# Two stacked transformer kinds on one core: the gated feed-forward hidden row made transposed, with head and end reordered

## The chip, the cores and the metric

The program runs on one core of one Trainium2 chip. The metric is the device time in microseconds of one execution; the lower, the better. TensorE is called PE, its weight load PEld, VectorE DVE, ScalarE ACT, GpSimd POOL and the DMA-issuing SyncE SP. L515 is line 515 of the kernel before.

## The reference, cut to what matters

A sequence of 256 rows of width 1024 goes through two layers of a first kind and then two layers of a second kind, everything in float32. Of a layer of the first kind only the feed-forward half is touched by the main part of the change (D_FF is 2816):

```python
def rms_norm(x, g):
    y = xf * lax.rsqrt(jnp.mean(xf * xf, axis=-1, keepdims=True) + EPS)
    return (y * g.astype(jnp.float32)).astype(x.dtype)
...
        x = x + jnp.concatenate([ret, da], axis=-1) @ w_out[l]
        h = rms_norm(x, ffn_norm_g[l])
        x = x + (jax.nn.silu(h @ w_gate[l]) * (h @ w_up[l])) @ w_down[l]
```

The second kind ends with `x = x + jnp.square(jax.nn.relu(hf @ w_up)) @ w_down` (its hidden width is 4096), and the program ends with a last rms norm. The row scale of a norm (the rsqrt) is one number for each of the 256 rows.

## The kernel before, in words

**Products.** Every float32 weight and activation is split into a high and a low part, and a product is the sum hi*hi + hi*lo + lo*hi. Weights come in slabs of 1 MB: 4 k-tiles of 128 by 512 columns (`w_raw`, `w_hi`, `w_lo`, a ring of 4). SP loads a slab as two DMAs when `lo_ready` says that the ring's place is free, ACT copies it to `w_hi` (`split_hi`, L1097), DVE subtracts for `w_lo` (`split_lo`, L1626), PE uses it. Three slabs are split ahead of their use (AHEAD = 3). The ACT and DVE programs are in-order lists in which the splits are written between the other work (`splits(n)`).

**Row-wise products** (`slab_product`, L515 to L517). The activations hT (transposed, hi and lo, k on the partitions) are stationary, the weights move, 512 columns at a time: for each k-tile and each of the two row halves three matmuls. The result has the sequence rows on its partitions. A block is an accumulation over all k-tiles into a pair of banks; there are two pairs, and `open_block` waits on `acc_free` until the block two before it has been read out.

**Transposed products** (`hidden`, L1032 to L1035), in the second kind only: the weights are stationary, and the moving operand is hi and lo of x side by side (512 columns) against the high weights, and x hi alone (256 columns) against the low weights. The result has hidden features on its partitions and the sequence along the columns. A bank then holds hi*hi plus the low-weight term in its left half and hi*lo in its right half: ACT copies the right half (`cross2`, L1563), DVE adds (`L2179`).

**The first kind's gated row before.** A wide block makes 256 gate columns and 256 up columns from two slabs (`gate_up` in SP's list: left half gate, right half up). ACT takes silu of the gate half with the row scale (L1342), DVE multiplies the up half by row scale and gate (L1904) into `hid1`. PE turns it with four transposes one block later (`turn_hid1`, L561), ACT takes the high part (L1120), DVE the low part (L1651). There are 11 wide blocks for each layer, then the down product over 22 k-tiles (6 slabs for each 512 columns), which `add_x` adds to x.

**Around it.** Before the gated row, w_out's product ends (`half_product`, L544 to L546). x's second half is added, turned by eight transposes (`turn_x(1)`), taken by ACT and DVE (L1127, L1655) and squared (L1137), DVE makes the mean (L1675), and POOL the reciprocal root (L2250), which is `rstd_ready`.

**Head.** After the constants have landed PE turns the gain rows, runs filler matmuls (`fill`, L631; a fill is two PE instructions), turns x's first half, runs a small sum, turns a group of convolution rows, and fills again; then the first projection starts (`first_pair`). Slab 0 is split in two halves. **End.** The last block is made one row half at a time; row half 0 is scaled by ACT (L1602), row half 1 by DVE in two pieces (L2234), and three DMAs write it out (SP L487, ACT L1604, SP L489).

Of the kernel before, what the change touches and what calls it, by code (L numbers as in the profile page):

```python
# [28 lines left out]
P = 128  # L29
# [9 lines left out]
FILLS = (4, 5, 4)  # L39
# [26 lines left out]
UPS = FF2 // HALF  # L66
BLOCKS1, BLOCKS2 = 7 + 2 + 11 + 2, 5 + 2 + 16 + 2 + UPS + 2
TURNS1, TURNS2 = 4 + 4 + 4 + 4 + 4 + 4 + 4 + 11 + 4 + 1, 2 + 1 + 1 + 10 + 12 + 1 + 1 + 4 + 4 + 4
assert not (BLOCKS1 % 2 or TURNS1 % 2 or TURNS2 % 2)
# [123 lines left out]
def build(nc, t, out):  # L193
    with ExitStack() as ctx:
# [60 lines left out]
        gate1 = over("gate1", [P, R, HALF], 44)  # L255
        hid1 = over("hid1", [P, R, HALF], 46)
# [62 lines left out]
        first_rest = sem("first_rest")  # L319
# [40 lines left out]
        cross_ready = sem("cross_ready")  # L360
        hid_ready = sem("hid_ready")
# [25 lines left out]
        def _(sp):  # L387
            q = Place(sp)
            sp.dma_start(x[:, 0, 0:NB], t["x"].rearrange("b (r p) d -> p (b r) d", p=P)[:, 0, 0:NB]).then_inc(x_in, 16)
# [22 lines left out]
            def halves(w, k0, c0):  # L412
                src = w[k0 * P:(k0 + 4) * P, bass.ds(c0, HALF)]
                return src.rearrange("(c p) n -> p c n", p=P)

            for l in q.layers(dict(slab=len(KTS1))):
                w = {n: t[n][bass.ds(l, 1)].rearrange("o k n -> (o k) n")
                     for n in ("w_in", "w_out", "w_gate", "w_up", "w_down")}
                for k0 in (0, 4):
                    for c0 in COLS1[:2]:  # L420
                        slab(*rows(w["w_in"], k0, 4, c0, NB))
                sp.wait_ge(first_rest, 1)
# [66 lines left out]
            sp.dma_start(rows_out[:, 1, 0:NB], outrow[:, 1, 0:NB]).then_inc(out_done, 16)  # L489
# [4 lines left out]
        def _(pe):  # L494
# [12 lines left out]
            def slab_product(a, hi, lo, kts, cols, first, last, halfway=None):  # L507
# [3 lines left out]
                for j, kt in enumerate(kts):  # L511
# [6 lines left out]
                    if j == 1 and halfway:  # L518
                        halfway()
# [64 lines left out]

            def first_block(product, cols=NB):
# [8 lines left out]
                product(a, hT_hi, hT_lo, range(0, 4), cols, True, False, turn_rest)  # L594
# [3 lines left out]
            def first_pair(product):  # L598
# [9 lines left out]
                def all_of_first():  # L608
                    pe.wait_ge(turn_free, turned_to + 1)
                    pe.wait_ge(first_rest, 1)  # L610

                product(a[0], hT_hi, hT_lo, range(0, 4), NB, True, False, all_of_first)
# [4 lines left out]
                for b in range(2):  # L617
                    product(a[b], hT_hi, hT_lo, range(4, 8), NB, False, True)

# [26 lines left out]
            for l in q.layers(dict(slab=len(KTS1), blk=BLOCKS1, turn=TURNS1, scores=16, dve=9)):  # L646
# [113 lines left out]
                first_pair(slab_product)  # L760
# [37 lines left out]
                def turn_hid1(blk):  # L798
                    read_out(blk)
                    turn_group([(hid1[:, r, c * P:(c + 1) * P], c * SEQ + r * P)  # L800
                                for c in range(2) for r in range(R)])
# [6 lines left out]
                earlier, last = q.now("turn"), q.now("blk")  # L808
                for b in range(2):
                    a = open_block()  # L810
                    for n in range(6):
# [3 lines left out]
                        if (b, n) == (0, 5):  # L815
                            all_turned()
# [1554 lines left out]
```

## Time and profile before

| what | value |
|---|---|
| median of 3 runs | 1441.19 us (1439.85 to 1441.36) |
| the profiled execution: its time | 1439.99 us |
| its span, first to last instruction | 1438.2 us |
| mean granted TensorE clock | 0.999 |
| PE / PEld / DVE / ACT / POOL busy | 99 / 82 / 65 / 52 / 7 % of the span |

The profiled execution's time is 1.8 us more than its span; the difference of a span is taken over to the time as it is. A matmul's own duration in the trace (0.39 us for 512 columns) overlaps with the next one; what one costs on PE is the distance from its start to the start of the next.

### The profile page before, as it was taken

Reading aid. Unit: us, or ns where it says so; the run is one execution under the profiler, and the core shown is the slowest. Engines: PE = TensorE matmul, PEld = TensorE weight load, DVE = VectorE, ACT = ScalarE, POOL = GpSimd, SP = SyncE. Lnnn points to the kernel's source line nnn. Section 1 sums busy time; section 2 is a strip of 40 time slices with the busy share of each in tenths; the row PEclk is TensorE's granted clock in tenths of the full one; section 3 lists DMA queues with packets and bytes.
Section 4 is the critical chain, followed back from the end, with each engine's and each line's share of the span. In section 5 each row is a group of like instructions: output and inputs, shape, how many; then the busy total and the mean of one; then the engine's idle time right before and its main releaser. Section 6 shows DMA issues by size and latency. Waiting matters only on the chain.

```text
span 1438.2 us, 19054 instructions
## 1 busy us (share of the span) xinstructions
PE 1425.9 (99%) x7027; PEld 1185.8 (82%) x7027; DVE 941.4 (65%) x1165; ACT 745.9 (52%) x994; POOL 100.0 (7%) x116
## 2 busy tenths in 40 slices
PE   8999999999999999999999999999999999999997
PEld 7788888888788888888888888888888888888886
DVE  6766655446757555446799878764467998787642
ACT  6665544345855444336665445544266654455431
POOL 1211000002111000000220000000002200000001
PEclk9999999999999999999999999999999999999999
DMA  8533755454434755465355566555553555665550
GB/s 336 176 119 117 234 179 198 165 189 163 158 118 149 231 175 182 168 205 187 126 184 175 184 205 208 200 180 201 175 186 127 183 176 184 205 207 200 181 187 29
DMA packets 172646, 257.11 MB, mean 179 GB/s; under 512 B 8478, under 2 KB 90400, under 8 KB 172448
## 3 DMA queue, kind: packets, MB, share of 16 engines
q1 hardware_dynamic: 169408, 249.36, 51.7%
q10 hardware_dynamic: 3023, 6.28, 1.3%
q8 instruction: 45, 0.74, 0.2%
q0 software_dynamic: 144, 0.52, 0.1%
q14 instruction: 26, 0.20, 0.0%
HBM read 255.08 MB, written 1.05 MB: 178 GB/s over the span
## 4 chain that ended last, share of the span: by engine, by line
PE 95%; POOL 1%; DVE 1%; issue 1%; ACT 1%; DMA 0%; POOLq 0%; DVEq 0%; ACTq 0%
PE bank L515 23%; PE bank L517 23%; PE bank L516 23%; PE bank L1033 8%; PE bank L561 4%; PE bank L1032 4%; PE bank L544 1%; PE bank L546 1%; PE bank L545 1%; PE bank L699 1%; POOL cst L2309 1%; PE bank L890 1%; PE bank L656 1%; PE bank L682 1%; PE bank L1035 1%
## 5 line engine op out<-in xcount | busy, mean ns | idle before, releaser
L1626 DVE TENSOR_TENSOR w_lo<-w_raw,w_hi 128x2048 fp32r<-128x2048 f32 (+2 forms) x247 | 538.3, 2184 | 215.8 <-ACT w_hi L1097 212.9
L1097 ACT CAST w_hi<-w_raw 128x2048 fp32r<-128x2048 f32 (+2 forms) x247 | 448.7, 1825 | 231.6 <-PE bank L517 207.8
L515 PE MATMUL bank<-w_hi,hT 128*128 128x512 f32 (+1 forms) x1056 | 417.7, 396 | 0.0
L517 PE MATMUL bank<-w_hi,hT 128*128 128x512 f32 (+1 forms) x1056 | 410.9, 389 | 0.0
L516 PE MATMUL bank<-w_lo,hT 128*128 128x512 f32 (+1 forms) x1056 | 410.1, 388 | 0.0
L517 PEld LDWEIGHTS bank<-w_hi,hT 128*128 128x128 f32 x1056 | 198.2, 188 | 41.2
L515 PEld LDWEIGHTS bank<-w_hi,hT 128*128 128x128 f32 x1056 | 198.4, 188 | 40.3 <-issue 2.5
L516 PEld LDWEIGHTS bank<-w_lo,hT 128*128 128x128 f32 x1056 | 198.6, 188 | 38.0
L1033 PE MATMUL bank<-hT,w_hi 128*128 128x512 f32 x512 | 178.2, 396 | 0.2
L1032 PE MATMUL bank<-hT,w_lo 128*128 128x256 f32 x448 | 125.2, 279 | 0.0
L1033 PEld LDWEIGHTS bank<-hT,w_hi 128*128 128x128 f32 x512 | 94.4, 188 | 21.0 <-DVE sum L2179 0.9
L2250 POOL TENSOR_TENSOR stat<-stat,cst 128x2 f32<-128x2 f32 (+4 forms) x24 | 44.8, 1869 | 959.6 <-DVE stat L1675 830.8
L515 PE MATMUL bank<-w_hi,hid2T_hi 128*128 128x512 f32 x240 | 93.5, 389 | 0.0
L517 PE MATMUL bank<-w_hi,hid2T_lo 128*128 128x512 f32 x240 | 93.4, 389 | 0.0
L516 PE MATMUL bank<-w_lo,hid2T_hi 128*128 128x512 f32 x240 | 93.4, 389 | 0.0
L1032 PEld LDWEIGHTS bank<-hT,w_lo 128*128 128x128 f32 x448 | 84.4, 188 | 1.3
L515 PE MATMUL bank<-w_hi,hid1T_hi 128*128 128x512 f32 x176 | 69.0, 392 | 0.0
L517 PE MATMUL bank<-w_hi,hid1T_lo 128*128 128x512 f32 x176 | 68.6, 389 | 0.0
L516 PE MATMUL bank<-w_lo,hid1T_hi 128*128 128x512 f32 x176 | 68.5, 389 | 0.0
L1120 ACT CAST hid1T_hi<-bank 128x512 f32 (+1 forms) x22 | 12.9, 587 | 90.3 <-PE bank L561 90.3
L1655 DVE SCALAR_TENSOR_TENSOR hT<-bank,gcols,hT 128x256 fp32r<-128x256 f32 (+1 forms) x72 | 32.6, 507 | 38.5 <-ACT hT L1127 35.5
L1563 ACT COPY cross<-bank 128x256 f32<-128x256 f32 x64 | 20.8, 377 | 70.8 <-PE bank L1033 70.8
(269 smaller groups left out, 1597.9 us busy)
## 6 DMA issues: line engine op xcount, KB each, us to landing
w_raw<-in_w_gate SPq DMA_DIRECT2D x108, 512.0 KB, 3.9
w_raw<-in_w_up SPq DMA_DIRECT2D x108, 512.0 KB, 4.5
w_raw<-in_w_down SPq DMA_DIRECT2D x104, 512.0 KB, 4.4
w_raw<-in_w_in SPq DMA_DIRECT2D x88, 512.0 KB, 4.6
w_raw<-in_w_out SPq DMA_DIRECT2D x16, 512.0 KB, 4.2
w_raw<-in_w_branch SPq DMA_DIRECT2D x32, 256.0 KB, 2.8
w_raw<-in_w_o SPq DMA_DIRECT2D x16, 512.0 KB, 4.5
bgate<-in_b_gate ACTq DMA_DIRECT2D x16, 256.0 KB, 3.4
```

Of the source, the lines that this page charges most:

```text
L515: pe.matmul(o, hi[:, kt, rows_of(r)], w_hi[:, s, j, 0:cols], start=begin, stop=False)
L516: pe.matmul(o, hi[:, kt, rows_of(r)], w_lo[:, s, j, 0:cols], start=False, stop=False)
L517: mm = pe.matmul(o, lo[:, kt, rows_of(r)], w_hi[:, s, j, 0:cols], start=False, stop=end)
L544: pe.matmul(a[r][:, :], hT_hi[:, kt, rows_of(r)], w_hi[:, s, j, :], start=begin, stop=False)
L561: tr = pe.transpose(b[0:m, col:col + n], src, ident[0:n, 0:n])
L1032: pe.matmul(o[:, 0:SEQ], lo[:, kt, cols], hT_hi[:, kt, :], start=False, stop=False)
L1033: mm = pe.matmul(o[:, :], hi[:, kt, cols], hT[:, :, kt, :], start=kt == 0, stop=kt == KT - 1)
L1097: act.copy(w_hi[:, s, 0:kts, :], w_raw[:, s, 0:kts, :]).then_inc(hi_ready, 1)
L1563: ins = act.copy(cross2[:, n, :], a[n][:, SEQ:2 * SEQ])
L1626: dve.tensor_tensor(w_lo[:, s, 0:kts, :], w_raw[:, s, 0:kts, :], w_hi[:, s, 0:kts, :].bitcast(F32), ALU.subtract).then_inc(lo_ready, 1)
L1655: return dve.scalar_tensor_tensor(lo, src, gain, hi.bitcast(F32), ALU.mult, ALU.subtract)
L2250: pool.tensor_tensor(dst, src, half[:, 0:n], ALU.pow).then_inc(rstd_ready, 1)
```

## The change

The gated row of the first kind is made by the transposed product that the second kind already uses. Gate and up become blocks of their own (22 blocks instead of 11 for each layer, one slab each, same bytes). The transposes of the hidden row go away. The gate's row scale, which now belongs along the columns, is laid out as a matrix: DVE spreads the row scale over 128 columns, PE turns it by two transposes in the middle of the first two blocks (`turn_scale`), DVE copies it to `scale1`. The up part's row scale is applied after the down product (`add_scaled`). In the head, slab 0 is loaded, split and used by single k-tiles, DMAs change queues, fillers go from (4, 5, 4) to (4, 2, 2), and some of ACT's and DVE's work changes place. At the end ACT scales half of row half 1.

```diff
-FILLS = (4, 5, 4)
+FILLS = (4, 2, 2)
...
 (SP)
-            sp.dma_start(x[:, 0, 0:NB], ...)
+            for r in range(R):
+                sp.dma_start(x[:, r, 0:NB], ...).then_inc(x_in, 16)
+            sp.dma_start(w_raw[:, 0, 1, :], ...).then_inc(slab_in[0], 16)
...
-                    for k0 in (0, 4):
-                        slab((lambda s: s[:, :, 0:HALF], halves(w["w_gate"], k0, c0)),
-                             (lambda s: s[:, :, HALF:NB], halves(w["w_up"], k0, c0)))
+                    for name in ("w_gate", "w_up"):
+                        src = w[name][:, bass.ds(c0, HALF)].rearrange("(c p) n -> p c n", p=P)
+                        slab((lambda s: narrow(s)[:, 0:4, :], src[:, 0:4, :]),
+                             (lambda s: narrow(s)[:, 4:8, :], src[:, 4:8, :]))
...
 (PE)
+                def next_of_first(j):
+                    if j == 1:
+                        pe.wait_ge(turn_free, turned_to + 1)
+                    if by_tiles and j < 3:
+                        pe.wait_ge(first_lo, j + 1)
...
+            def first_hidden(between):
+                all_turned()
+                last = q.now("blk")
+                first = [(open_block(), up_slab())]
+                hidden(*first[0], range(0, 4))
+                read_out(last)
+                turn_x(1)
+                first.append((open_block(), up_slab()))
+                hidden(*first[1], range(0, 4))
+                turned_to = q.now("turn")
+                for g in range(2):
+                    pe.wait_ge(turn_free, turned_to + 1 + g)
+                    for opened in first:
+                        hidden(*opened, range(4 + 2 * g, 6 + 2 * g))
+                    if g == 0 and between:
+                        between()
...
+            fill(FILLS[2])
             pe.wait_ge(rows_in, 16)
             turn_group([(crows[0:65, l, :], l * 65) for l in range(DEPTH)])
-            fill(FILLS[2])
...
-                first_block(slab_product)
-                for _i in q.rounds(5, dict(slab=4, blk=2, turn=2)):
-                    for _ in range(2):
-                        wide_block()
-                        turn_hid1(q.now("blk") - 1)
+                def turn_scale():
+                    pe.wait_ge(scale_ready, l + 1)
+                    turn_group([(scale_rows[:, r, :], r * P) for r in range(R)])
+                first_hidden(turn_scale)
+                for _i in q.rounds(5, dict(slab=4, blk=4)):
+                    for _ in range(4):
+                        hidden_block()
...
 (ACT)
-            act.dma_start(x[:, 1, 0:NB], ...)
-            act.dma_start(crows[0:65, :, :], ...)
+            for kt, landed in ((0, tile_in[0]), (2, tile_in[1]), (3, slab_rest_in[0])):
+                act.dma_start(w_raw[:, 0, kt, :], ...).then_inc(landed, 16)
...
             act.wait_ge(turn_free, 3)
+            first_slab_hi(0, tile_in[0]).then_inc(first_hi, 1)
             take_model((0, 1), 0)
...
+            act.wait_ge(x_in, 32)
+            square_x(0)
+            act.wait_ge(slab_in[1], q.next("in1", 16))
+            act.copy(w_hi[:, 1, 0:2, :], w_raw[:, 1, 0:2, :]).then_inc(second_hi, 1)
+            act.wait_ge(slab_rest_in[1], q.now("in1"))
+            act.copy(w_hi[:, 1, 2:4, :], w_raw[:, 1, 2:4, :]).then_inc(hi_ready, 1)
-            for _ in range(AHEAD - 1):
+            for _ in range(AHEAD - 2):
                 split_hi()
...
+                for i in q.rounds(5, dict(loop4, blk=4, cross=4, hid1=2)):
                     for j in range(2):
+                        cross_of_first()
+                        split_hi()
                         gate()
+                        cross_of_first()
                         split_hi()
-                        split_hi()
-                        take_hi(hid1T_hi[:, bass.ds(i * 4 + 2 * j, 2), :])
+                        hidden1_hi(i * 4 + 2 * j)
...
             act.activation(outrow[:, 0, :], outrow[:, 0, :], ACT.Copy, scale=rstd[0]).then_inc(out_ready, 1)
+            act.activation(outrow[:, 1, 0:NB], outrow[:, 1, 0:NB], ACT.Copy, scale=rstd[1]).then_inc(out_ready, 1)
...
 (DVE, head: the first slab by tiles, then the second by halves, then the five small angle steps that stood before)
+            dve.wait_ge(first_hi, 1)
+            slab_lo(0, slice(0, 1)).then_inc(lo_ready, 1)
             take_model((0, 1), 0)
...
 (DVE, gated row)
+                def gate():
+                    sum_of_first(gate1)
+                    dve.tensor_tensor(gate1[:, :, :], gate1[:, :, :], scale1[:, :].unsqueeze(1).to_broadcast([P, 2, SEQ]),
+                                      ALU.mult).then_inc(gate_sum, 1)
                 def up():
+                    sum_of_first(sum1)
+                    dve.wait_ge(act_done, q.next("act_done"))
+                    dve.tensor_tensor(sum1[:, :, :], sum1[:, :, :], gate1[:, :, :], ALU.mult).then_inc(hid1_ready, 1)
...
-                splits(3)
+                splits(2)
                 root()
+                for r in range(R):
+                    ins = dve.tensor_scalar(scale_rows[:, r, :], cst[:, C_ONE:C_ONE + P], rstd[r], None, ALU.mult)
+                ins.then_inc(scale_ready, 1)
+                dve.tensor_copy(scale1[:, :], next_turn()[:, 0:SEQ]).then_inc(turn_free, 1)
...
                     for j in range(2):
+                        gate()
+                        split_lo()
                         up()
                         split_lo()
-                        split_lo()
-                        take_lo(hid1T_lo[...], hid1T_hi[...])
+                        hidden1_lo(i * 4 + 2 * j)
...
 (POOL)
+            pool.dma_start(crows[0:65, :, :], ...).then_inc(rows_in, 16)
             pool.wait_ge(x_in, 32)
             pool.dma_start(x[:, :, NB:D], ...).then_inc(x_rest_in, 16)
```

## Rows read from the trace of the kernel before

**Rows 1.** The page: busy shares, and the chain that ended last by engine.

```profile
PE 1425.9 (99%) x7027; PEld 1185.8 (82%) x7027; DVE 941.4 (65%) x1165; ACT 745.9 (52%) x994; POOL 100.0 (7%) x116
...
PE 95%; POOL 1%; DVE 1%; issue 1%; ACT 1%; DMA 0%; POOLq 0%; DVEq 0%; ACTq 0%
```

**Rows 2.** Waits of PE, the longest of three: us in total, times, longest.

```profile
PE bank L631 <- DVE ones L1707: 1.5, 1, 1.5
```

**Rows 3.** Timeline of PE, the first layer's gated row: start, duration, instruction.

```profile
139.12 0.39 PE L515 MATMUL bank<-w_hi,hT 128*128 128x512 f32 x1
...
161.78 0.60 PE L561 MATMUL bank<-cst,hid 128*128 128x128 f32 x4
...
264.04 0.60 PE L561 MATMUL bank<-cst,hid 128*128 128x128 f32 x4
264.40 0.48 PE L515 MATMUL bank<-w_hi,hid1T_hi 128*128 128x512 f32 x1
```

**Rows 4.** Timeline of PE, first transposed blocks of the second kind.

```profile
856.88 0.39 PE L1033 MATMUL bank<-hT,w_hi 128*128 128x512 f32 x1
...
859.69 1.03 PE L561 MATMUL bank<-cst,x 128*128 128x128 f32 x8
...
866.20 0.28 PE L1032 MATMUL bank<-hT,w_lo 128*128 128x256 f32 x1
...
868.79 1.02 PE L1033 MATMUL bank<-hT,w_hi 128*128 128x512 f32 x2
869.65 0.28 PE L1035 MATMUL bank<-hT,w_lo 128*128 128x256 f32 x1
```

**Rows 5.** Timeline of ACT, steady transposed blocks; the two copies are eight blocks apart.

```profile
903.20 0.65 ACT L1563 COPY cross<-bank 128x256 f32<-128x256 f32 x2 [2.59 <-PE bank L1033]
...
947.98 0.65 ACT L1563 COPY cross<-bank 128x256 f32<-128x256 f32 x2 [2.59 <-PE bank L1033]
```

**Rows 6.** Timeline of DVE, start of the first layer's gated row.

```profile
143.35 1.66 DVE L1655 SCALAR_TENSOR_TENSOR hT<-bank,gcols,hT 128x256 fp32r<-128x256 f32 x4 [0.55 <-ACT hT L1127]
...
145.72 6.69 DVE L1626 TENSOR_TENSOR w_lo<-w_raw,w_hi 128x2048 fp32r<-128x2048 f32 x3
```

**Rows 7.** Timelines of ACT and POOL, same stretch.

```profile
145.44 3.73 ACT L1097 CAST w_hi<-w_raw 128x2048 fp32r<-128x2048 f32 x2
...
145.89 2.67 POOL L2250 TENSOR_TENSOR stat<-stat,cst 128x2 f32<-128x2 f32 x1 [20.22 <-DVE stat L1675]
```

**Rows 8.** DVE groups by shape: count, busy us, mean ns, idle before.

```profile
L1626 DVE TENSOR_TENSOR w_lo<-w_raw,w_hi 128x2048 fp32r<-128x2048 f32 x223 | 509.9, 2291 | 215.2 <-ACT w_hi L1097 212.9 <-DVE comb L1786 1.5 <-DVE uT L2025 0.3
...
L1969 DVE TENSOR_SCALAR soft<-soft,stat 128x128 f32<-128x128 f32 x24 | 6.9, 287 | 0.9
```

**Rows 9.** The chain in order of time, head: start, us, what.

```profile
4.93 2.20 PE bank L631 x10
...
8.02 0.85 ACT hT L1127 x2
8.89 0.89 DVE hT L1655 x2
...
10.22 0.95 PE bank L631 x8
```

**Rows 10.** Timeline of PE, head: starts of the first and third projection piece.

```profile
11.19 0.47 PE L515 MATMUL bank<-w_hi,hT 128*128 128x512 f32 x1
...
23.10 0.39 PE L515 MATMUL bank<-w_hi,hT 128*128 128x512 f32 x1
```

**Rows 11.** Timeline of DVE, head.

```profile
16.63 2.29 DVE L1626 TENSOR_TENSOR w_lo<-w_raw,w_hi 128x2048 fp32r<-128x2048 f32 x1 [0.87 <-ACT w_hi L1097]
...
19.51 1.66 DVE L1655 SCALAR_TENSOR_TENSOR hT<-bank,gcols,hT 128x256 fp32r<-128x256 f32 x4
```

**Rows 12.** Timeline of the end: the last scalings and DMA issues.

```profile
1432.72 1.15 ACT L1602 ACTIVATE w_raw<-w_raw,stat 128x1024 f32<-128x1024 f32 x1 [0.56 <-POOL stat L2250]
...
1434.30 0.43 SPq L489 DMA_DIRECT2D out<-w_raw  x1
```

More of the change, by code:

```diff
@@ L419, in _ @@
                 for k0 in (0, 4):
-                    for c0 in COLS1[:2]:
-                        slab(*rows(w["w_in"], k0, 4, c0, NB))
-                sp.wait_ge(first_rest, 1)
+                    for n, c0 in enumerate(COLS1[:2]):
+                        if (l, k0, n) == (0, 0, 0):
+                            sp.wait_ge(lo_ready, q.next("slab"))
+                        else:
+                            slab(*rows(w["w_in"], k0, 4, c0, NB))
+                if l == 0:
+                    sp.wait_ge(first_lo, 3)
                 for c0 in COLS1[2:]:
@@ L618, in first_pair, with up_slab, hidden, hidden_block @@
                     product(a[b], hT_hi, hT_lo, range(4, 8), NB, False, True)
+            def up_slab():
+                pe.wait_ge(lo_ready, q.next("slab") + RING)
+                return (q.index("slab") - 1) % RING
+            def hidden(a, slab, kts):
+                hi, lo = narrow(w_hi[:, slab]), narrow(w_lo[:, slab])
+                for kt in kts:
+                    for n in range(2):
+                        o, cols = a[n], slice(n * P, (n + 1) * P)
+                        if kt:
+                            pe.matmul(o[:, 0:SEQ], lo[:, kt, cols], hT_hi[:, kt, :], start=False, stop=False)
+                        mm = pe.matmul(o[:, :], hi[:, kt, cols], hT[:, :, kt, :], start=kt == 0, stop=kt == KT - 1)
+                        if not kt:
+                            pe.matmul(o[:, 0:SEQ], lo[:, kt, cols], hT_hi[:, kt, :], start=False, stop=False)
+                if kt == KT - 1:
+                    mm.then_inc(slab_used, 1)
+            def hidden_block():
+                a = open_block()
+                hidden(a, up_slab(), range(KT))
+            def first_hidden(between):
[14 more added lines that the diff above has]
+                        between()
             def turn_pair(qsrc, ksrc):
@@ L1373, in _ @@
                         **{f"in{s}": 16 * len(KTS2) // RING for s in range(RING)})
-            for l in q.layers(per2, dict(slab=AHEAD, turn=2, **{f"in{s}": 16 for s in range(AHEAD)})):
+            for l in q.layers(per2, dict(used=8, slab=AHEAD, turn=2, **{f"in{s}": 16 for s in range(AHEAD)})):
                 ahead = iter(KTS2[AHEAD:] + KTS2[:AHEAD])
@@ L1587, in _ @@
                 splits(6 if l < DEPTH - 1 else 6 - AHEAD)
-                used(8)
+                if l < DEPTH - 1:
+                    used(8)
                 block_of()
@@ L1897, in _, with sum_of_first @@
                 take_x1(l * 16 + 8)
-                def up():
-                    used(2)
+                def sum_of_first(dst):
+                    used(1)
+                    a = block_of()
+                    dve.wait_ge(cross1_ready, q.next("cross"))
+                    for n in range(2):
+                        ins = dve.tensor_tensor(dst[:, n, :], a[n][:, 0:SEQ], cross1[:, n, :], ALU.add)
+                    ins.then_inc(acc_free, 1)
+                    dve.wait_ge(acc_free, q.now("blk") + 2)
@@ L1921, in _ @@
-                splits(7)
+                gate()
+                splits(1)
+                up()
+                splits(1)
+                hidden1_lo(20)
+                splits(6)
                 used(6)
-                add_x(0)
+                add_scaled(0)
                 splits(1)
```

218 lines of the change are left out of this document (105 added, 113 removed).

## Prediction

> **What bounds the kernel now.** I read the page first. PE is busy 99% of the span and holds 95% of the chain that ended last [rows 1], so the end is set by the sum of PE's starts, plus the few places where PE waits. The list of PE's waits has three lines, all in the first 10 us, 3.6 us in all (1.5, 1.2 and 0.9), the longest of them in [rows 2]. So from the first projection to the last matmul nobody keeps PE waiting for long, and an edit on DVE or ACT is worth nothing unless it makes PE wait or takes one of these waits. The reader has to look at three stretches: the gated row of each first-kind layer, the head up to the third projection piece, and the 8 us behind the last matmul.
>
> **The transposed product itself.** One gate+up block before has 48 matmuls of 512 columns and four transposes. Its period is (264.04 - 161.78) / 9 = 11.36 us [rows 3]. Two transposed blocks do the same product; in the second kind eight of them take 947.98 - 903.20 = 44.78 us, 5.60 us each, 11.20 us for two [rows 5]. The columns streamed are the same (2 x 16 x 768 against 48 x 512), so the transposed form is no cheaper in columns. What it saves is the transposes, and it gives part of that back in the pace of its mixed matmuls: 0.17 us for each of 11 blocks.
>
> The whole row of a layer: before, 139.12 to 264.40 is 125.28 us, with ten groups of transposes in it; the eleventh stands in the down product and costs its 0.36 us and about 0.1 on the matmul behind it (0.48 where others show 0.39) [rows 3], so 125.74. After, the first two blocks with their eight transposes of x and the short wait before the third block go as in the second kind: 869.65 - 856.88 = 12.77 us [rows 4]. The other twenty take 20 x 5.60 = 111.95. The two transposes of the row scale are new: half of 0.36, and 0.1 behind them, 0.28. Sum 125.00, which is 0.74 less than before, 1.5 us less for both layers. Bounds: if the stretch ran at the pace of the plain form with no extra at all, two blocks would take 11.36 - 0.46 = 10.90 and the layer would win 3 us more; if a wait like that before the third block (869.65 against a start near 869.2, 0.45 us) came back often, it would lose as much. I take the measured period, since the instructions, banks and slabs are those of the second kind.
>
> The Trainium skill, page "TensorE: Matmul & The Clock Gate", section "Back-to-back issue gap", puts a matmul of N columns at N/2.4 + 2.5 ns on the warm clock. By it 48 matmuls of 512 take 10.36 us and the 64 of two transposed blocks 10.40, and the removed transposes would be nearly all gain. The rows of this kernel do not agree: two transposed blocks take 11.20 us.
>
> **The wait that comes in: the row scale.** PE may not turn the scale before DVE has written `scale_rows`. PE's instructions are in order, so everything behind `turn_scale`, the last quarter of the first two blocks included, is queued behind it. When does PE get there? In the second kind this place lies 866.20 - 856.88 = 9.32 us behind the start [rows 4], so at 139.12 + 9.32 = 148.4 in the first layer. When is DVE there? Its queue is: take x's second half (143.35 to 145.0), mean, then two weight splits, then the root, then two small operations. The second half of x is turned 0.1 us later than before (2.81 us behind the start [rows 4]), so the splits begin at 145.8 instead of 145.72. Three took 6.69 us [rows 6], two take 4.46: 150.3. ACT has their high parts by then (casts from 145.44, 3.73 us for two, of which the first is used [rows 7]). POOL's root is done by 148.6 at the latest [rows 7], so it is hidden by the splits; without them it would be the next to be late, by 0.2 us. Two DVE operations of 128x128 at 0.287 [rows 8], partly overlapped, 0.5: 150.8. PE waits 2.4 us in each layer, 4.8 in both. Bounds: nothing, if the order of splits and root left DVE free at 148.4; 3 us, if the handoffs add up.
>
> Together the gated rows cost -1.5 + 4.8 = +3.3 us.
>
> **Covered work.** In the loop, for two blocks (11.2 us), DVE has two sums (0.76 each), two products (0.69), two splits (2.29 [rows 8]) and one low part (0.68): 8.2 us. ACT has two copies (0.65), two splits (1.9 [rows 7]), silu and high part (0.65 each): 6.4 us. Both fit under PE, and a block has 5.6 us to be read out; the cover is gone at +3 us on DVE. The row scale's copy and `add_scaled` (0.75 instead of 0.68 us) lie beside matmuls. SP issues the same bytes in the same pieces. The last hidden tiles are needed by the sixth slab of the down product, over 25 us after they are begun.
>
> **Head.** The chain before runs: fills 4.93 to 7.13, x turned, ACT 8.02, DVE 8.89 to 9.78, turn of the rows, fills 10.22 for 0.95 us, first projection at 11.19 [rows 9, 10]. The edits drop the last fills from the chain (-0.95) and six PE fill instructions, 1.3 us, before x; there x's landing (POOL, which waits for it, is let go at 6.4) and ACT's extra quarter split (about 0.6 us) then set the pace, so that the first projection starts 1 to 1.9 us earlier. But that is not kept. The third piece needs all of x's second half, which DVE takes at 19.51 to 21.17 [rows 11], 1.9 us before PE asks for it at 23.10 [rows 10]. In DVE's queue before that now stand: slab 1, which waits for ACT, whose squares (1.5 us) were moved ahead of it, done near 15.7; five or six small angle steps moved behind it (about 1.5 us); slab 2 (2.2), four small operations (0.75), and then x (1.66), which ends near 22.0. So DVE becomes the bound of the head, and the third piece starts at 22.05 instead of 23.10: -1.0 us. Bounds: 0 (x or the convolution rows, now fetched by POOL's queue, land late) and -1.9.
>
> **End.** ACT's row half 0 runs 1432.72 to 1433.87 [rows 12]; its new piece of 512 columns (0.6) ends at 1434.5 and its DMA goes out behind it. Before, the last DMA went out at 1434.30. +0.1 us, bounds -0.2 and +0.3.
>
> **Sum.** +3.3 - 1.0 + 0.1 = +2.4 us. On the profiled execution's own time, 1439.99 (span 1438.2 and 1.8 around it), that is 1442.4; that execution lies 1.2 below the median of the runs, 1441.19, on which the forecast is 1443.6 us. A measurement of this kernel can tell about 0.2%, 2.9 us, from no change; +2.4 is inside.
>
> **Rivals.**
> - *The scale is there in time* (chance 0.15): DVE's splits run earlier than I place them. Then -1.5 - 1.0 + 0.1 = -2.4: 1438.8. For it: POOL's root ends near PE's need. Against: three splits stand back to back behind the mean in [rows 6], and two of them remain.
> - *The head gives nothing* (0.12): +3.4, 1444.6. For it: the head lives from DMA landings, and x's second half was moved behind another transfer of POOL.
> - *The clock falls in the new wait* (0.08): PE stands still for over 2 us twice. No gap after the head in this trace is that long, and the granted clock was 0.999. At the slower level a fill took 0.22 us (2.20 for 10), at the faster 0.12 (0.95 for 8) [rows 9]; 3 us of work at the slower level costs 1.5 more, so about +3 for two layers: 1446.6.
> - *DVE or ACT falls behind in the loop* (0.08): a wait of 0.1 us at each of 40 blocks is +4: 1447.6. Against it: 3 us of slack in 11.2.
> - *The page's pace* (0.03): two transposed blocks at 10.40 against 10.36 and the whole 0.46 us of transposes saved would make each layer win 0.42 x 11 = 4.6 instead of 0.74, so 1436.
> - The forecast keeps 0.54, with its own range of 1442.0 to 1445.0.
>
> **How the numbers follow.** The range takes in the first rival at its lower end and the clock's at its upper: 1438.8 to 1446.6. Faster by over 0.2% (below 1438.3): half of the first rival at most and the page's pace, 0.10. Slower (above 1444.1): the late head, the clock, the loop, and a fifth of the forecast's own case, 0.36. Within: 0.54.
>
> **What would show it.** PE's waits get a new line: the transposes of the scale wait for DVE's `scale_rows`, 2 times, 2.4 us each. The gated row, from w_out's last matmul to the first of the down product, takes 127.4 us where it took 125.3; the steady pair of blocks 11.20. The third projection piece starts near 22.05, right behind DVE's taking of x. If the wait for the scale is absent, the largest step is wrong; if the steady pair is not 11.20, the reading of the second kind doesn't carry over; if the stretch behind the wait shows doubled distances, the clock has fallen.

## The result and the profile after

The changed kernel takes 1443.59 us (median of 20 runs, 1441.84 to 1444.25); the kernel before, measured beside it, takes 1439.99 us (20 runs, 1439.75 to 1441.58). The ratio is 1.0021, 95% interval [1.0015, 1.0028]: 3.0 us slower, clear of no change. The two medians lie 3.6 us apart; the ratio is smaller because 7 of the 20 runs of before stand in a group of their own at 1441.19 to 1441.58, which the median does not see. The forecast was +2.4 us and 1443.6. That the absolute figure was met to 0.01 us is luck: the forecast stood on the first three of these runs of before, whose median of 1441.19 lies 1.2 us above that of all 20, and its difference is 1.2 us below that of the medians. The difference is the better test.

The profiled execution has a span of 1442.0 us against 1438.2, so 3.8 us are to be found in the two traces. First PE's busy share and the chain by engine [rows 1]:

```profile
PE 1426.2 (99%) x7285; PEld 1195.5 (83%) x7285; DVE 987.3 (68%) x1261; ACT 768.8 (53%) x1064; POOL 100.9 (7%) x117
...
PE 94%; DVE 2%; POOL 1%; issue 1%; ACT 1%; DMA 0%; ACTq 0%; SPq 0%; POOLq 0%; DVEq 0%
```

PE works 0.3 us longer than before and the span is 3.8 longer, so nearly all of it is PE standing still; matmuls at a slower pace count as busy, and some of those are found below. PE's waits name the place (us in total, times, longest). The lines for the scale, for x and for the gate are new; before's 1.2 us for x's first tiles on DVE is gone [rows 2]:

```profile
PE bank L575 <- DVE scale_rows L1997: 3.9, 2, 2.0
...
PE bank L575 <- DMA x<-in_x: 0.5, 1, 0.5
PE bank L654 <- DVE gate L1966: 0.2, 1, 0.2
```

**The first layer's gated row.** Timeline of PE, from the row's start to the down product [rows 3]:

```profile
139.08 0.39 PE L654 MATMUL bank<-hT,w_hi 128*128 128x512 f32 x1
...
148.39 0.40 PE L654 MATMUL bank<-hT,w_hi 128*128 128x512 f32 x1
150.70 0.44 PE L575 MATMUL bank<-cst,scale_rows 128*128 128x128 f32 x2 [1.91 <-DVE scale_rows L1997]
...
154.16 0.51 PE L654 MATMUL bank<-hT,w_hi 128*128 128x512 f32 x1 [0.20 <-DVE gate L1966]
...
266.13 0.39 PE L529 MATMUL bank<-w_hi,hid1T_hi 128*128 128x512 f32 x1
```

The row takes 266.13 - 139.08 = 127.05 us where it took 125.28. DVE in the same stretch [rows 6] shows why PE stood still for 1.91 us: two weight splits lie between the root's input and `scale_rows`.

```profile
145.76 4.49 DVE L1676 TENSOR_TENSOR w_lo<-w_raw,w_hi 128x2048 fp32r<-128x2048 f32 x2
150.17 0.47 DVE L1997 TENSOR_SCALAR scale_rows<-cst,stat 128x128 f32<-128x128 f32 x2
```

The steady pair of blocks, from ACT's copies of cross two blocks apart [rows 5], is 171.23 - 160.03 = 11.20 us, as forecast:

```profile
160.03 0.65 ACT L1373 COPY cross<-bank 128x256 f32<-128x256 f32 x2 [0.42 <-PE bank L654]
...
171.23 0.65 ACT L1373 COPY cross<-bank 128x256 f32<-128x256 f32 x2 [2.62 <-PE bank L654]
```

**The second layer's.** The same wait, and then something the first layer does not show. Timeline of PE:

```profile
454.72 0.39 PE L654 MATMUL bank<-hT,w_hi 128*128 128x512 f32 x1
...
466.34 0.58 PE L575 MATMUL bank<-cst,scale_rows 128*128 128x128 f32 x2 [1.99 <-DVE scale_rows L1997]
...
467.36 0.41 PE L653 MATMUL bank<-hT,w_lo 128*128 128x256 f32 x1
...
468.00 0.41 PE L653 MATMUL bank<-hT,w_lo 128*128 128x256 f32 x1
...
470.26 0.28 PE L653 MATMUL bank<-hT,w_lo 128*128 128x256 f32 x1
...
470.62 0.28 PE L653 MATMUL bank<-hT,w_lo 128*128 128x256 f32 x1
...
583.13 0.40 PE L529 MATMUL bank<-w_hi,hid1T_hi 128*128 128x512 f32 x1
```

A pair of matmuls takes 468.00 - 467.36 = 0.64 us there and 470.62 - 470.26 = 0.36 at the end. The windows view of this stretch (busy us of PE, its weight loads, DVE, ACT, POOL; the last three figures are granted clock, DMA share, GB/s) has the granted clock at the 1.2 GHz level for the first two microseconds and back at the 2.4 GHz level after four:

```profile
467.00:469.00 2.00, 2.00 (x8) 1.71 (x8) 0.38 (x1) 0.00 (x0) 0.00 (x0) 0.50 1.08 378
469.00:471.00 2.00, 2.00 (x10) 1.53 (x8) 0.77 (x3) 1.48 (x3) 0.00 (x0) 0.77 1.07 369
471.00:473.00 2.00, 2.00 (x12) 1.69 (x12) 1.67 (x2) 2.00 (x5) 0.00 (x0) 1.00 0.19 66
```

This row takes 583.13 - 454.72 = 128.41 us, 1.36 more than the first layer's.

**The head.** Timeline of PE [rows 9, 10]:

```profile
6.38 1.97 PE L575 MATMUL bank<-cst,x 128*128 128x128 f32 x8 [0.52 <-DMA x<-in_x]
...
9.99 0.77 PE L529 MATMUL bank<-w_hi,hT 128*128 128x512 f32 x1
...
11.41 0.63 PE L529 MATMUL bank<-w_hi,hT 128*128 128x512 f32 x1
11.84 0.63 PE L530 MATMUL bank<-w_lo,hT 128*128 128x512 f32 x1
...
12.63 0.39 PE L529 MATMUL bank<-w_hi,hT 128*128 128x512 f32 x1
12.85 0.40 PE L530 MATMUL bank<-w_lo,hT 128*128 128x512 f32 x1
...
23.06 0.39 PE L529 MATMUL bank<-w_hi,hT 128*128 128x512 f32 x1
```

The first projection starts 1.2 us earlier than before (9.99 against 11.19), but its matmuls stand 0.43 us apart (11.41 to 11.84) until about 12.5, and 0.22 to 0.23 from then on. 0.43 us for 512 columns is the 1.2 GHz level: in the second layer's slow stretch, where the granted clock is 0.50, they stand as far apart. The Trainium skill, page "TensorE: Matmul & The Clock Gate", section "Back-to-back issue gap", gives N/1.2 on that level, 0.427 us, and the rows agree. The 1.2 us are spent by the third piece, which starts at 23.06 against 23.10. The two executions are not alike in this, though: in that of before the eight fills ahead of the first projection took 0.95 us [rows 9], the pace of the 2.4 GHz level. What the head gives between executions that are alike is worked out behind the experiments. DVE has its x ready by then (19.75 to 21.41):

```profile
19.75 1.66 DVE L1705 SCALAR_TENSOR_TENSOR hT<-bank,gcols,hT 128x256 fp32r<-128x256 f32 x4
```

**The end** is unchanged: from the start of the last 512-column matmul (1433.95; before 1430.17) to the end of the span it is 8.05 us, before 8.03.

**The sum of the traces.** From layer 1's gated row to layer 2's: 454.72 - 139.08 = 315.64 us against 453.56 - 139.12 = 314.44, +1.20. From layer 2's to the last matmul: 979.23 against 976.61, +2.62. Head -0.04, end 0. That is the 3.8 us.

### The profile page after: what moved, and what is told of

It is laid out like the page before. It is cut to its first block, busy times and chain, and to the rows that moved or that the text cites. A ratio compares the mean times of both kernels' runs of the same rounds, so it can differ in the third digit from the quotient of the medians.

```text
span 1442.0 us, 19813 instructions
## 1 busy us (share of the span) xinstructions
PE 1426.2 (99%) x7285; PEld 1195.5 (83%) x7285; DVE 987.3 (68%) x1261; ACT 768.8 (53%) x1064; POOL 100.9 (7%) x117
## 3 DMA queue, kind: packets, MB, share of 16 engines
HBM read 255.08 MB, written 1.05 MB: 178 GB/s over the span
## 4 chain that ended last, share of the span: by engine, by line
PE 94%; DVE 2%; POOL 1%; issue 1%; ACT 1%; DMA 0%; ACTq 0%; SPq 0%; POOLq 0%; DVEq 0%
PE bank L654 19%; PE bank L529 18%; PE bank L531 18%; PE bank L530 18%; PE bank L653 8%; PE bank L575 4%; PE bank L656 1%; PE bank L558 1%; PE bank L560 1%; PE bank L559 1%; PE bank L761 1%; POOL cst L2402 1%; DVE w_lo L1676 1%; PE bank L945 1%; PE bank L718 1%
## 5 line engine op out<-in xcount | busy, mean ns | idle before, releaser
L1676 DVE TENSOR_TENSOR w_lo<-w_raw,w_hi 128x2048 fp32r<-128x2048 f32 (+1 forms) x246 | 536.8, 2185 | 176.4 <-ACT w_hi L1118 173.4
L1118 ACT CAST w_hi<-w_raw 128x2048 fp32r<-128x2048 f32 (+1 forms) x246 | 447.8, 1827 | 195.0 <-PE bank L531 171.0
L654 PE MATMUL bank<-hT,w_hi 128*128 128x512 f32 x1216 | 423.9, 397 | 0.4 <-DVE gate L1966 0.2
L653 PE MATMUL bank<-hT,w_lo 128*128 128x256 f32 x1064 | 298.0, 280 | 0.0
L529 PE MATMUL bank<-w_hi,hT 128*128 128x512 f32 (+1 forms) x704 | 279.3, 397 | 0.0
L531 PE MATMUL bank<-w_hi,hT 128*128 128x512 f32 (+1 forms) x704 | 273.9, 389 | 0.0
L530 PE MATMUL bank<-w_lo,hT 128*128 128x512 f32 (+1 forms) x704 | 273.5, 388 | 0.0
L654 PEld LDWEIGHTS bank<-hT,w_hi 128*128 128x128 f32 x1216 | 224.6, 188 | 50.1 <-issue 1.2
L653 PEld LDWEIGHTS bank<-hT,w_lo 128*128 128x128 f32 x1064 | 201.2, 189 | 3.2
L531 PEld LDWEIGHTS bank<-w_hi,hT 128*128 128x128 f32 x704 | 132.4, 188 | 27.3
L529 PEld LDWEIGHTS bank<-w_hi,hT 128*128 128x128 f32 x704 | 132.7, 188 | 27.0 <-issue 2.3
L530 PEld LDWEIGHTS bank<-w_lo,hT 128*128 128x128 f32 x704 | 132.7, 188 | 24.9
```

What stands on the lines that cost most here:

```text
L529: pe.matmul(o, hi[:, kt, rows_of(r)], w_hi[:, s, j, 0:cols], start=begin, stop=False)
L530: pe.matmul(o, hi[:, kt, rows_of(r)], w_lo[:, s, j, 0:cols], start=False, stop=False)
L531: mm = pe.matmul(o, lo[:, kt, rows_of(r)], w_hi[:, s, j, 0:cols], start=False, stop=end)
L653: pe.matmul(o[:, 0:SEQ], lo[:, kt, cols], hT_hi[:, kt, :], start=False, stop=False)
L654: mm = pe.matmul(o[:, :], hi[:, kt, cols], hT[:, :, kt, :], start=kt == 0, stop=kt == KT - 1)
L1118: act.copy(w_hi[:, s, 0:kts, :], w_raw[:, s, 0:kts, :]).then_inc(hi_ready, 1)
```

## The experiments

Eleven kernels ran: ten others, and the changed one again. "The gated row" is the stretch measured above, and its two lengths are those of layers 1 and 2 in the profiled execution. The changed kernel, experiments 1 to 4, 5 to 8 and 9 to 11 were measured at four different times; each ratio is to runs of before taken beside it, whose median was 1439.99, 1440.03, 1439.95 and 1440.21 us.

**1. The gated row alone.** The head's, the end's and the fillers' hunks are taken back; the rest of the change stays.

```diff
-FILLS = (4, 2, 2)
+FILLS = (4, 5, 4)
...
(head of SP, ACT, DVE, POOL and the last scalings as in the kernel before)
```

> The transposed gated row on the kernel before, head and end left as they were. Theory (the wait for the row scale, with the clock at its slower level behind it in one layer, is the whole loss): each gated row about 1.3 us longer by the wait of 2 us less the 0.7 us of transposes, and 1.5 us more where the clock falls, so +2.6 to +4.5 us against the kernel before. Rival (the head carries part of the loss): +1.0 to +2.0 only.

Measured 1444.07 us, ratio 1.0026 [1.0015, 1.0036]. Its waits for `scale_rows` are 3.9 us, two times, as in the whole change. Its rows take 128.19 and 127.01 us, so that here the *first* layer is the long one. Timeline of PE there:

```profile
152.32 0.44 PE L567 MATMUL bank<-cst,scale_rows 128*128 128x128 f32 x2 [1.99 <-DVE scale_rows L1964]
...
153.07 0.40 PE L645 MATMUL bank<-hT,w_hi 128*128 128x512 f32 x1
...
153.42 0.39 PE L645 MATMUL bank<-hT,w_hi 128*128 128x512 f32 x1
...
154.39 0.63 PE L645 MATMUL bank<-hT,w_hi 128*128 128x512 f32 x1
...
155.03 0.63 PE L645 MATMUL bank<-hT,w_hi 128*128 128x512 f32 x1
```

A pair takes 153.42 - 153.07 = 0.35 us behind the restart and 155.03 - 154.39 = 0.64 later; the change comes at about 153.8, 1.5 us behind the wait. So the gated row makes the slowdown, and the fall of the clock belongs to neither layer. The median is 4.0 us above before's beside it, inside the theory's range and far from the rival's.

**2. Head and end alone.** The gated row as before, all other hunks in.

```diff
-FILLS = (4, 5, 4)
+FILLS = (4, 2, 2)
...
(gated row of PE, ACT, DVE, SP and add_scaled as in the kernel before)
```

> Head and end of the change on the kernel before, the gated row left as it was. Theory (the head starts its first projection 1.2 us earlier but runs it at the clock's slower level, the end gives nothing): 0, within 0.7 us. Rival (the head's gain of 1.0 us is real and hidden by noise in the one trace): -1.0 to -1.5 us. Forecast of the prediction: -0.9.

Measured 1440.19 us, ratio 0.9999 [0.9989, 1.0008]: over all runs worth nothing that can be told. Its profiled execution is a short one (1438.64, span 1436.8): there x's second half is turned at 14.62 instead of 16.76, and the third piece starts at 21.39 instead of 23.10. Only one other run is as short (1438.43); the other nine lie between 1439.50 and 1440.96, while 23 of the 30 runs of before beside them lie in the lower of its two groups (1439.62 to 1440.40). So the median does not settle between theory and rival: the gain is real in this execution, and most runs do not show it.

**3. The scale ahead of the second split.** The changed kernel, with one DVE split moved behind `scale_rows`.

```diff
-                splits(2)
+                splits(1)
                 root()
                 for r in range(R):
                     ins = dve.tensor_scalar(scale_rows[:, r, :], cst[:, C_ONE:C_ONE + P], rstd[r], None, ALU.mult)
                 ins.then_inc(scale_ready, 1)
+                splits(1)
                 dve.tensor_copy(scale1[:, :], next_turn()[:, 0:SEQ]).then_inc(turn_free, 1)
```

> The change, with one DVE split moved behind the writing of the row scale, so that it is ready near 148.6 instead of 150.65. Theory: the wait shrinks from about 2.2 to under 0.4 us in each layer and the clock no longer falls behind it: 3.5 to 5.5 us faster than the change, 0 to -2 against the kernel before. Rival (POOL's root is late, 2.67 us behind the mean): the wait only shrinks by 1.5 to 1.9 us. Rival (the loss is in the pace of the transposed blocks): no gain over 0.5 us.

Measured 1439.41 us, ratio 0.9992 [0.9983, 1.0001]: 4.2 us below the changed kernel. Rows 125.53 and 125.58 us, together 4.4 less than in the changed kernel, no matmul of them at doubled distance. Timeline of PE, then of DVE in the same stretch:

```profile
147.42 0.44 PE L575 MATMUL bank<-cst,scale_rows 128*128 128x128 f32 x2 [0.47 <-DVE scale_rows L1997]
```

```profile
144.01 2.29 DVE L1676 TENSOR_TENSOR w_lo<-w_raw,w_hi 128x2048 fp32r<-128x2048 f32 x1
146.89 0.48 DVE L1997 TENSOR_SCALAR scale_rows<-cst,stat 128x128 f32<-128x128 f32 x2 [0.59 <-POOL stat L2344]
```

With one split fewer ahead, POOL's root is the next to be late, by 0.59 us of DVE's time. The two waits shrink from 3.9 to 0.8 us in all, 1.5 for each layer: the rival that names POOL is right on the wait, the theory on the total.

**4. The wait filled.** The changed kernel; PE multiplies the identity with itself 8 times (16 PE instructions) into a bank that is free, ahead of its wait. DVE is untouched, so the scale is as late as before.

```diff
                 def turn_scale():
+                    for _ in range(8):
+                        pe.matmul(score[1][:, 0:P], ident, ident, start=True, stop=True)
                     pe.wait_ge(scale_ready, l + 1)
```

> The change, with 8 filler matmuls of 128 columns (16 PE instructions, about 1.9 us) into an unused bank before PE waits for the row scale. Theory (PE's idling there lets the clock fall in one layer): the stretch at the slower level is gone, the wait is replaced by the fillers: 1.0 to 1.5 us faster than the change in executions in which the clock fell, so 0.5 to 1.5 in the median. Rival (the slower stretch comes of something else): same as the change or up to 0.3 us slower, and the doubled distances stay.

Measured 1442.18 us, ratio 1.0011 [1.0002, 1.0020]. Timeline of PE:

```profile
146.90 1.95 PE L863 MATMUL bank<-cst 128*128 128x128 f32 x16
149.05 0.44 PE L575 MATMUL bank<-cst,scale_rows 128*128 128x128 f32 x2 [0.20 <-DVE scale_rows L1999]
```

Rows 127.12 and 127.03: the same lost time as in the changed kernel's first layer, and no slow stretch in either. So of the 4.2 us between the changed kernel and experiment 3, 1.4 come from the clock (1443.59 to 1442.18) and 2.8 from the wait itself. The rows agree: both layers together go from 255.5 to 254.2 us with the fillers and to 251.1 in experiment 3, 1.3 and 3.0.

**5, 6. More fillers in the head**, in the kernel of experiment 3.

```diff
-FILLS = (4, 2, 2)
+FILLS = (4, 3, 2)     (experiment 5)
+FILLS = (4, 4, 4)     (experiment 6)
```

> The kernel of the experiment with the scale ahead of the second split (median 1439.4), with three fillers instead of two ahead of x (two more PE instructions, 0.22 us each at the slower level). Theory A, the head is set by when the granted clock rises, and that is decided by the gap in which PE waits for x: the gap (0.5 us) closes, the clock is at the faster level by x's transposes in every execution, and the median goes to about 1438.0. Rival B, the moment of the rise varies by itself from one execution to the next: the median stays at 1439.4 within 0.5. Rival C, the fillers only push x's transposes back: +0.2, 1439.6.

> The same kernel, with four fillers ahead of x and four where the clock gate is filled for the third time, in place of two and two (eight more PE instructions). Theory A (a filled head raises the clock early each time): 1438.0 or a little less, and all executions within 1 us. Rival B (the rise varies by itself): 1439.4 within 0.5, executions spread over 2 us as before. Rival C (the fillers lie on the chain): 0.4 us ahead of x and 0.5 us ahead of the first projection, about 1440.3.

Measured 1439.48, ratio 0.9994 [0.9985, 1.0003], and 1438.53, ratio 0.9988 [0.9979, 0.9997]. One more filler ahead of x did nothing that can be told: the runs still spread from 1437.66 to 1440.00. In its profile, as in experiment 3's, no gap stands ahead of x's transposes, and both executions are short ones; experiments 7, 8 and 11 show a late clock without the gap. So the gap is not what decides. With fillers in both places ten of the eleven runs lie within 1437.90 to 1438.77, the eleventh at 1440.01. In its profiled execution the fills and x's transposes are at the slower level nearly up to the projection, and the projection, which starts at 10.75, is at the faster from its first matmul:

```profile
8.96 1.85 PE L693 MATMUL bank<-ones 128*128 128x128 f32 x8
...
10.75 0.48 PE L529 MATMUL bank<-w_hi,hT 128*128 128x512 f32 x1
11.06 0.39 PE L530 MATMUL bank<-w_lo,hT 128*128 128x512 f32 x1
```

**7. The turn one block later.** The kernel of experiment 3, `turn_scale` between the two blocks of the last quarter.

```diff
-                    for opened in first:
+                    for n, opened in enumerate(first):
                         hidden(*opened, range(4 + 2 * g, 6 + 2 * g))
-                    if g == 0 and between:
-                        between()
+                        if (g, n) == (1, 0) and between:
+                            between()
```

> The same kernel as with the scale ahead of the second split, and the turn of the scale on PE stands one block later, between the two blocks of the first round's last quarter instead of ahead of them. Theory A (what is left of the price of the scale is PE standing behind scale_rows, 0.4 us in the first layer): that wait is gone, the gate then waits 0.2 to 0.4 us instead, and the time is 1439.2 within 0.4. Rival B (the gate needs the scale soon after, so the wait only moves to the third block): the third block starts later by what the turn was put back, 0.7 us a layer, and the time is 1440.8.

Measured 1438.43, ratio 0.9987 [0.9978, 0.9996]. The wait for `scale_rows` is gone, the third block's for the gate is 0.7 us in each layer (0.2 before), and the rows take 125.32 and 125.42, 0.19 less on average than in experiment 3. Layer 1's gated row to layer 2's takes 453.31 - 139.40 = 313.91 us, 0.53 less than before the change. The wait has moved to the third block, as rival B said, but costs less than it did. The rows account for 0.4 of the 1.0 us between the medians of experiments 3 and 7, which ran at different times; the rest is not explained.

**8. A longer wait.** The changed kernel, with two reductions on DVE ahead of `scale_rows`.

```diff
                 splits(2)
                 root()
+                for r in range(R):
+                    dve.tensor_reduce(gate1[:, r, 0:1], x[:, r, 0:1024], AX.X, ALU.max)
```

> The changed kernel, with two reductions of 128x1024 (about 1.1 us each) put on DVE ahead of scale_rows, so that PE waits about 4.2 us instead of 2 in each layer; the numbers they give are not used. Theory A (a wait costs its own length, and beyond a length the granted clock falls behind it and costs 1.5 us more): waits of about 4.2 us, +4.4 for both layers, and slower starts behind both of them, so +4.4 +1.5 (the layer that kept its clock in the profile of the changed kernel), about 1449.5. Rival B (the fall of the clock has nothing to do with the wait's length): +4.4 alone, about 1448.0, with doubled distances behind one wait or none.

Measured 1449.61, ratio 1.0064 [1.0051, 1.0078], +6.0 us on the changed kernel: 2 x 2.2 us more wait, and the clock in the layer that had been spared. Windows view, first layer, then the timeline of the second:

```profile
152.00:154.00 2.00, 1.50 (x6) 1.41 (x7) 0.87 (x4) 0.00 (x0) 0.00 (x0) 0.57 1.07 372
```

```profile
471.80 0.69 PE L575 MATMUL bank<-cst,scale_rows 128*128 128x128 f32 x2 [4.14 <-DVE scale_rows L1999]
...
472.49 0.63 PE L654 MATMUL bank<-hT,w_hi 128*128 128x512 f32 x1
...
473.13 0.63 PE L654 MATMUL bank<-hT,w_hi 128*128 128x512 f32 x1
```

Rows 130.69 and 131.03. The waits are 4.25 and 4.14 us, and both layers restart at the slower level (a granted clock of 0.57 from 152 to 154 us, where PE restarts at 152.50, in layer 1; 0.64 us a pair in layer 2). Theory A was right.

**9. The placed row with the old head and end.** Experiment 1 with the two edits of experiments 3 and 7.

> The kernel before with the transposed gated row alone, the scale ahead of the second split on DVE and its turn one block later on PE; head and end as before. Theory A (the row itself gives back what its two waits cost): both layers together come out 0.5 us each below before, as in the kernel that has head and end too (layer 1's start to layer 2's start took 313.91 us there, 314.44 before), so 1439.0. Rival B (what was gained with the head's and end's edits came from these): no gain, 1440.0.

Measured 1440.12, ratio 0.9993 [0.9984, 1.0002]: as a median this is theory B's number. The trace says otherwise. Rows 125.32 and 125.42, layer to layer 454.38 - 140.47 = 313.91, 0.53 less than before, as theory A says. What hides it is the head of that execution, where the clock rose late, some 13.4 us into the span. Timeline of PE:

```profile
10.20 2.02 PE L684 MATMUL bank<-ones 128*128 128x128 f32 x8
11.87 0.77 PE L521 MATMUL bank<-w_hi,hT 128*128 128x512 f32 x1
...
12.87 0.62 PE L523 MATMUL bank<-w_hi,hT 128*128 128x512 f32 x1
13.30 0.43 PE L521 MATMUL bank<-w_hi,hT 128*128 128x512 f32 x1
```

The eight fills that took 0.95 us [rows 9] take 2.02, x's second half is turned at 18.11 instead of 16.76, and the third piece starts at 24.46 instead of 23.10. The runs fall into two groups, 1438.78 to 1439.07 (five) and 1440.12 to 1440.76 (six); those of before, beside them, into 1439.85 to 1440.63 (17) and 1441.16 to 1441.88 (10). Group against group the row is 1.0 to 1.2 us faster; the medians are mixtures of the two. That the upper group is the late clock is read from one profiled execution on each side (1440.42 here, late; 1439.99 of before, early), and from the distance of the groups, which is that of the third pieces, 1.4 us.

**10. Both placements and the fills.** Experiment 7 with `FILLS = (4, 4, 4)`.

> All of the change, the scale ahead of the second split, its turn one block later, and the fills 4, 4 and 4. Theory A (the two gains add up: 0.4 us from the turn's place, and fewer late rises of the clock in the head from the fills): 1438.1, with a small spread. Rival B (either gave its gain in the same executions, or by luck): 1438.5.

Measured 1437.54 us (11 runs, 1437.27 to 1438.34), ratio 0.9980 [0.9971, 0.9989]. It beats both kernels: 2.7 us under before (1440.21 beside it), 6 under the changed one (experiment 11, beside it). All runs lie within 1.1 us; there is no second group. Theory A has the direction and undersized the gain by 0.6 us.

**11. The changed kernel again.**

> The changed kernel as it is, beside the others on one chip: 1443.6 within 0.4; and in its profile a wait of 2 us for scale_rows in each layer. If the fall of the clock behind a wait of this length varies from one execution to the next, it may be found behind the first layer's wait, behind the second's, behind both or none; if it belongs to the second layer, it is there again and alone.

Measured 1443.51, ratio 1.0018 [1.0009, 1.0027]. Waits 3.9 us, two times; the slow stretch again in the second layer alone (row 128.18, first layer 127.13). Its head had no gap ahead of x (transposes at 5.79), and yet its matmuls stand at the slower distance until 12.95. One of the eleven runs is at 1440.72, the rest between 1443.27 and 1443.75. Not tried, and so open: what in an execution decides when the clock rises in the head.

## Why the prediction was right, and where it was not

**The new wait: right in place and cause, oversized.** Forecast 2 x 2.4 us behind `scale_rows`, measured 1.91 and 1.99, 3.9 in all instead of 4.8. DVE was done 0.2 us earlier than forecast (150.6 against 150.8). The rest is the way of counting: the forecast counts from the *start* of PE's last matmul (148.39), the profile from its end (148.79). By the distance of starts the next could have begun at 148.39 + 0.23, so that the first layer loses 2.1 us and the term is too large by 0.3 for each layer. In experiment 3 the two rows lose 4.4 us of their length (1.3 of it the clock) by moving one split; experiment 4 keeps the lost time and shows that filling it gains only the clock.

**The transposed row itself: right.** Without its wait layer 1 comes to 1.20 - 1.91 = -0.71 us by the profile's count of the wait, and to 1.20 - 2.08 = -0.88 by starts, where -0.74 was forecast; steady pair 11.20. The rival at 1436, 4.6 us for each layer, is ruled out by this. Well placed, the row earns 0.5 us a layer net of the 0.7 us that its third block still waits.

**The clock: a rival at 0.08 that came half true.** The forecast's argument against it was that the average granted clock was 0.999 and no such gap stood in the trace; that says nothing about a gap that did not exist yet. The fall came behind one of the two waits in each profiled execution (changed kernel twice, experiment 1), and cost 1.36 us in the trace (128.41 - 127.05; 1.05 and 1.18 in the other two) and 1.4 in the medians (experiment 4). The forecast's price for it, 1.5 for each layer, was a little high; the 3 us of slow work in it came from no row and turned out near (466.34 to about 469.9). Its chance was too low.

**The head: the step that failed.** The forecast put -1.0 us there, with DVE as the new bound and the third piece at 22.05; it starts at 23.06. The step counted six fewer fill instructions ahead of x and the last fills as time saved (1.3 and 0.95 us), and put at nothing what they do for the clock: it took for granted that the clock rises as early as in the one trace of before. In the profiled executions of this case it rises early or late, and the third piece follows it. The moment of the rise is the trace's first record of the full clock:

| head | clock rises at | third piece starts at |
|---|---|---|
| before's, early (before) | 7.72 | 23.10 |
| changed, early (experiments 2, 3, 4) | 7.70, 8.54, 8.17 | 21.39, 21.09, 21.19 |
| before's, late (experiments 1, 9) | 13.82, 13.36 | 24.66, 24.46 |
| changed, late (after; experiments 7, 8, 11) | 12.54; 13.84, 12.35, 13.04 | 23.06; 23.35, 22.62, 22.99 |

The other three have other fills (experiments 5, 6 and 10: 8.54, 10.45 and 8.13). Like against like the new head is 1.7 to 2.0 us ahead where the clock rises early and 1.1 to 2.0 where it rises late, so its edits do give what was forecast and more. A late rise costs the new head 1.2 to 2.3 us and the old one 1.4 to 1.6. The zero between the two profiled executions is an early one of before against a late one of the changed kernel. Timeline of PE, third piece of the old head with a late rise, experiment 1:

```profile
24.66 0.39 PE L521 MATMUL bank<-w_hi,hT 128*128 128x512 f32 x1
```

Early, the new head is the forecast's. Timeline of PE, then of DVE, in the profiled execution of experiment 4, whose head is that of the changed kernel:

```profile
21.19 0.51 PE L529 MATMUL bank<-w_hi,hT 128*128 128x512 f32 x1 [0.27 <-DVE hT L1707]
```

```profile
19.48 1.66 DVE L1707 SCALAR_TENSOR_TENSOR hT<-bank,gcols,hT 128x256 fp32r<-128x256 f32 x4
```

DVE bounds the third piece, and it is done with x at 21.14 where the forecast had 22.0: 1.9 us are gained, the lower bound given. Late, the projection at the slower pace is the bound (DVE is done at 21.41, PE comes at 23.06). What takes the gain away over the medians is how often each kind comes. Before's runs stand in the lower group 13 of 20, 23 of 30 and 17 of 27 times; with the new head and its two fills only 2 of 11 runs of experiment 2 and 2 of 11 of experiment 3 are as short as the profiled early one, and 18 of the changed kernel's 20 lie above 1442.9. That the fills have to do with it is seen where they alone were put back: ten of eleven runs at or below 1438.77 in experiment 6, four in experiment 5 beside it, and all eleven within 1.1 us in experiment 10. They are not the whole of it, since 6 of 11 runs of experiment 9 are of the longer kind with all of the old fills. Most runs have no trace, so the shares are read from their times; that they moved because of the fills is likely, not shown. By the ratios, head and end were worth 0 (experiment 2), -0.7 (changed kernel against experiment 1) and -0.9 us (experiment 7 against 9), none of it clear of noise; the rival "the head gives nothing" (0.12) describes the changed kernel's median best, though not for its reason, late landings.

**The end: 0** instead of +0.1.

**The sum.** Forecast 4.8 - 1.5 - 1.0 + 0.1 = +2.4. By the traces 3.9 - 1.5 + 1.4 + 0 = +3.8, and by the ratio +3.0. The wait and the end were put too high by 1.0, the clock and the head too low by 2.4; the errors cancel in part, and against the ratio the total is off by 0.6 us, less than its parts. A slip in the chances changes nothing: the parts listed for "slower" add to 0.39, not 0.36.

## What to carry to other kernels

When a change makes PE need a small result of another engine, look at what stands in that engine's queue ahead of it; here splits in the wrong place cost 3.9 us of waits and 1.4 of clock for a gain of 1.5, and moving one of them gave most of it back. Price a new PE wait with the clock behind it, not by its length alone. And before counting a gain at the start of a kernel, look at the pace of the first matmuls: executions whose clock rises late need their own sum, compare them only with their like, and ask whether the edit changes how often they come. A median over both kinds hid more than 1 us here.

## What the runs showed of the hardware

- A wait of 2.0 us in PE's otherwise full stream was followed by the 1.2 GHz level in one layer of two in three profiled executions, once only 1.5 us after PE had restarted (about 153.8, behind a restart at 152.32). Waits of 4.1 to 4.3 us were followed by it in both layers. Waits of 0.2 to 0.8 us never were, nor, in either layer of one execution, was a lost time of some 2.15 us of which 1.95 were filled with small matmuls.
- The slow stretch behind a wait was some 3 us long and, behind a wait of 2.0 us, cost 1.1 to 1.4 us; in the second layer of experiment 8 it ran from 471.8 to about 476.5.
- The first rise of the clock came at 7.7 to 8.5 us in six profiled executions, at 10.45 in one and at 12.4 to 13.8 in six. With the same head and nearly the same start of x's transposes it came at 8.17 (experiment 4, transposes at 5.68) and at 12.35 (experiment 8, at 5.70).
- In the head, the windows view gives a granted clock of 1.00 in the very stretch of the changed kernel where 512-column matmuls stand 0.43 us apart:

```profile
10.00:12.00 2.00, 2.00 (x8) 1.61 (x7) 2.00 (x6) 1.97 (x7) 0.00 (x0) 1.00 1.06 421
```

The trace's first record of the clock is the rise at 12.54, and the view counts the time ahead of it as full; the mean of 0.999 of before leaves out its slow first 7.7 us in the same way. There the distances have to be read, not the clock's column.
